# Re-spacing the mixing steps between the expert rows of a two-layer decoder on one Trainium2 core

## The chip, the core and the metric

The kernel runs on one core of one Trainium2 chip. The metric is the time of the whole launch in microseconds on the device: 1575.68 us for the kernel before, the median of three runs (1574.5 to 1578.08). TensorE, VectorE, ScalarE, GpSimd and SyncE are called PE, DVE, ACT, POOL and SP, as in the profile.

## The reference, cut to what matters

Two layers over 256 tokens of width 1024 (two tiles of 128 tokens). Each layer first mixes tokens (pooling and attention, gated, projected), then retrieves for each token 8 x 16 = 128 single-neuron experts from a table of 16384 and adds their outputs.

```python
def hybrid_layer(x, ...):
    h = rmsnorm(x, g_mix)
    z = h @ w_in                                  # pooling input, q, k, v, gate logits
    merged = gates[..., :D_MODEL] * branch_a + gates[..., D_MODEL:] * branch_b
    x = x + merged @ w_out
    return x + peer_ffn(rmsnorm(x, g_ffn), ...)

def peer_ffn(x, w_q, sub_keys, u, v):             # for each chunk of 128 tokens
    q = (xc @ w_q).reshape(TOKEN_CHUNK, PEER_HEADS, 2, PEER_HALF)
    s = jnp.einsum('thpd,pkd->thpk', q, sub_keys)
    sv, si = lax.top_k(s, PEER_TOPK)              # 16 best keys of each half
    ...                                           # 16 best sums give the expert ids eid and g
    act = jax.nn.gelu(jnp.einsum('thkd,td->thk', u[eid], xc))
    y = jnp.einsum('thk,thkd->td', g * act, v[eid])
```

## The kernel before

The work is four **windows** (layer 0 tile 0, layer 0 tile 1, layer 1 tile 0, layer 1 tile 1). A window's retrieval is 128 **rows**. Row g brings, for each of the 128 tokens, one expert's u and v vectors (2048 floats a token, 1 MiB a row) into one of the 7 slots of `ring`. Two rows make a **tick**, 64 ticks make a window, so there are 512 rows and 256 ticks.

What a row passes through:
- POOL issues an indirect DMA (line 1316), in order. It first waits until the slot's previous user, row g-7, has been summed.
- DVE computes the dot product with `tok` (`dot`, line 1181), ACT turns it into a weight through a GELU (lines 877 to 885).
- The v half is then summed in one of two ways. Row 0 of a tick listed in the set `shared` is summed on DVE (`weighted`, line 1194), behind the other row's dot. Every other row is summed on PE: ACT writes a diagonal (line 895), PE multiplies with it into two accumulating banks (`tensor_row`, line 675). That count, 382 rows on PE and 130 on DVE, is the same with and without the change.

The **mixing** of window w+1 and the search for its experts are cut into steps and slipped between the rows of window w. Each engine has a generator of steps for each window (`tensor_mix`, `scalar_mix`, `scalar_tops`, `vector_mix`); a step yields the tick at which it is due, and `streamed` emits row after row and, behind each, every step that has come due. So the order on each engine is fixed when the program is built. `when(w, tick)` turns a window's own tick into a tick of the program:

```python
def when(w, tick):
    return TICKS * (w - 1) + MIX_START + tick
```

The steps that matter here, with their ticks in `CHUNK_TICKS` and elsewhere:
- Ticks 5 to 26: projections with 1 MiB weight chunks (q, k, v, pooling input, gates, attention output), line 476 and others. SP loads chunks into two slots of `wring`; a load waits until the chunk two places earlier has been used. Twelve chunks of a layer stay in `held`.
- Ticks 31 to 35.5: output projection. `EASY` names ticks around it that are in `shared`.
- Ticks 42 to 63, every 3: eight **queries** pq0 to pq7 (line 476, 16 matmuls each, then two `score` matmuls, line 649, two ticks later). Behind pq5, PE spreads the gain row over all partitions (`everywhere`, line 398), which `hand_over` needs.
- `later_heads`: eight **heads** on DVE. Each has six steps: key search (lines 924 to 930) in two parts, search of the sums (lines 938 to 952) in two parts, picking of the ids (lines 971 to 985) in two parts.

Window 0's own steps have literal ticks (`first_heads`, `first_queries`).

At the first tick of a window (64, 128, 192) DVE runs `hand_over` (line 1173), which makes the new window's `tok` from x and the spread gain, ahead of the window's first dot; and behind the second dot `close` (line 1202) adds the PE banks to the old window's x. PE waits for `close` before it sums rows of the new window.

```python
def vector_row(dve, t, r):
    w, n = t // TICKS, t % TICKS
    if r == 0:
        for was in rows_on_vector(t - 1) if t else ():
            weighted(dve, t - 1, was)
        if n == 0:
            hand_over(dve, w)
    dot(dve, 2 * t + r)
    if r and n == 0 and w:
        close(dve, w - 1)
```

## Time and profile before

| what | value |
|---|---|
| median of three runs | 1575.68 us (1574.5 to 1578.08) |
| the profiled execution's own time | 1575.04 us |
| its span | 1573.3 us |
| PE, DVE, ACT, POOL busy | 82%, 73%, 58%, 42% of the span |
| moved by DMA | 643.51 MB, 409 GB/s over the span |
| first expert row's load | 103 us after the start |

The page gives busy shares of each engine, then the span in 40 slices with the rate of the DMA engines. The view of windows gives the same for stretches of one's own choice. The timeline lists instructions in order: start, length, engine, line, what it writes and reads, how often, and in brackets how long the engine had been idle before it and what ended that. All times are microseconds from the start of the span.

### The profile page before, as it was taken

The page shows a single profiled execution, that of the slowest core. Times are in us where ns is not written, and L with a number is a line of the kernel's source. Part 1 is how long each engine was busy: PE and PEld are TensorE (multiplying, and loading weights), DVE is VectorE, ACT ScalarE, POOL GpSimd, SP SyncE. Part 2 cuts the span into 40 slices and gives each one's busy share as a digit, 9 for nine tenths or more (in the row PEclk, how much of TensorE's full clock was granted, in tenths as well). Part 3 has the DMA queues.
Part 4 walks back from the last instruction along what each step waited for, and adds up shares of the span by engine and source line. Part 5 has one row for each costly group of instructions (what it writes and reads, how often), then busy time and mean ns, then how long its engine had stood idle before and what let it go on. Part 6 is the DMA issues. An engine that isn't in the chain of part 4 may idle for free.

```text
span 1573.3 us, 18796 instructions
## 1 busy us (share of the span) xinstructions
PE 1284.6 (82%) x5582; PEld 788.0 (50%) x5582; DVE 1149.6 (73%) x2692; ACT 914.3 (58%) x3307; POOL 662.0 (42%) x516
## 2 busy tenths in 40 slices
PE   8999898886898788766688978797778888787875
PEld 8986566543554556533355546564445542222321
DVE  2159998877888869636778887976778777777545
ACT  2236566557667546434676664655676666666676
POOL 0014344455445333223554433335554445554552
PEclk9999999997999899986899989999999999999999
DMA  9979999999999999999999999999999999999997
GB/s 393 397 320 401 408 413 420 421 421 422 402 389 408 421 420 421 421 421 419 421 417 410 396 417 422 419 420 421 421 418 416 396 410 421 421 421 421 421 420 292
DMA packets 89742, 643.51 MB, mean 409 GB/s; under 512 B 9976, under 2 KB 10536, under 8 KB 11816
## 3 DMA queue, kind: packets, MB, share of 16 engines
q0 software_dynamic: 73728, 536.90, 82.8%
q1 hardware_dynamic: 15588, 105.18, 16.2%
q8 instruction: 44, 0.72, 0.2%
q14 instruction: 58, 0.48, 0.1%
q10 hardware_dynamic: 324, 0.23, 0.0%
HBM read 641.23 MB, written 1.05 MB: 408 GB/s over the span
## 4 chain that ended last, share of the span: by engine, by line
DMA 43%; PE 26%; DVE 18%; ACT 6%; issue 5%; POOL 2%; SPq 0%; DVEq 0%; POOLq 0%; ACTq 0%
DMA ring<-in_uv,expert 41%; PE ybank L675 13%; PE bank L476 9%; DVE ring L1181 7%; DVE xs L1194 2%; POOL ring L1316 2%; DMA wring<-in_chunks 2%; PE bank L622 1%; ACT wgt L885 1%; ACT diag L895 1%; PE bank L611 1%; ACT th L883 1%; DVE buf L974 1%; DVE picked L977 1%; DVE si L930 1%
## 5 line engine op out<-in xcount | busy, mean ns | idle before, releaser
L1316 POOL DMA_INDIRECT ring<-in_uv,expert x512 | 661.8, 1293 | 890.8 <-PE ybank L675 546.2
L675 PE MATMUL ybank<-ring,diag 128*128 128x512 f32 x1528 | 790.7, 653 | 260.7 <-ACT diag L895 259.8
L1181 DVE SCALAR_TENSOR_TENSOR ring<-ring,tok 128x1024 f32<-128x1024 f32 x512 | 624.4, 1224 | 311.3 <-DMA ring<-in_uv,expert 305.8
L675 PEld LDWEIGHTS ybank<-ring,diag 128*128 128x128 f32 x1528 | 282.4, 200 | 654.6 <-ACT diag L895 417.7
L877 ACT ACTIVATE sq<-dots 128x1 f32<-128x1 f32 x512 | 102.8, 201 | 512.2 <-DVE ring L1181 511.2
L885 ACT ACTIVATE wgt<-th,half_p 128x1 f32<-128x1 f32 x512 | 198.1, 387 | 17.1
L476 PEld LDWEIGHTS bank<-hT,wring 128*128 128x128 f32 x1536 | 186.0, 199 | 35.1 <-issue 31.0
L476 PE MATMUL bank<-hT,wring 128*128 128x128 f32 x1536 | 186.8, 282 | 8.4 <-DMA wring<-in_chunks 8.1
L1194 DVE SCALAR_TENSOR_TENSOR xs<-ring,wgt,xs 128x1024 f32<-128x1024 f32 x128 | 164.0, 1282 | 5.2 <-ACT wgt L885 3.7
L895 ACT ACTIVATE diag<-cst,wgt 128x128 f32<-128x128 f32 x382 | 153.4, 402 | 15.9 <-PE ybank L675 3.6
L883 ACT ACTIVATE th<-arg,dots 128x1 f32<-128x1 f32 x512 | 150.8, 295 | 16.6
L878 ACT ACTIVATE half_p<-dots,prob 128x1 f32<-128x1 f32 x512 | 142.8, 279 | 0.2
L880 ACT ACTIVATE arg<-sq,gelu_bias 128x1 f32<-128x1 f32 x512 | 142.9, 279 | 0.0
L476 PEld LDWEIGHTS bank<-hT,held 128*128 128x128 f32 x736 | 91.5, 202 | 13.5 <-issue 13.5
L476 PE MATMUL bank<-hT,held 128*128 128x128 f32 x736 | 90.6, 284 | 0.0
L622 PE MATMUL bank<-held,buf 128*128 128x256 f32 x256 | 59.0, 385 | 0.0
L622 PEld LDWEIGHTS bank<-held,buf 128*128 128x128 f32 x256 | 49.9, 196 | 13.8 <-issue 7.4
L476 PE MATMUL bank<-hT,ring 128*128 128x128 f32 x448 | 51.1, 276 | 0.2 <-DMA ring<-in_chunks 0.2
L476 PEld LDWEIGHTS bank<-hT,ring 128*128 128x128 f32 x448 | 50.4, 192 | 0.9 <-DMA ring<-in_chunks 0.6
L686 ACT ACTIVATE buf<-bank 128x256 f32<-128x256 f32 (+2 forms) x65 | 28.5, 446 | 32.8 <-PE bank L476 30.1
L1181 DVE DVE_READ_ACCUMULATOR ring<-ring,tok 128x1 f32 x512 | 42.1, 82 | 0.0
L930 DVE FIND_INDEX8 si<-sv,buf 128x8 uint32<-128x128 f32 x128 | 34.9, 284 | 0.0
(126 smaller groups left out, 791.8 us busy)
## 6 DMA issues: line engine op xcount, KB each, us to landing
wring<-in_chunks SPq DMA_DIRECT2D x52, 1024.0 KB, 9.6
held<-in_chunks SPq DMA_DIRECT2D x24, 1024.0 KB, 24.8
ring<-in_chunks SPq DMA_DIRECT2D x20, 1024.0 KB, 12.0
ring<-in_uv,expert POOLq DMA_INDIRECT x512, 11.9
xs<-in_x SPq DMA_DIRECT2D x2, 512.0 KB, 4.3
wpool<-in_w_pool SPq DMA_DIRECT2D x2, 512.0 KB, 13.4
trunk_out<-buf SPq DMA_DIRECT2D x4, 256.0 KB, 4.8
ring<-in_pool_scale SPq DMA_DIRECT2D x1, 512.0 KB, 14.3
```

Source lines behind the costliest of these rows:

```text
L476: ins = pe.matmul(b[:, m * CW + lo:m * CW + lo + P], wt[k][:, lo:lo + P], hT[:, k, :], start=(k == 0), stop=(k == KC - 1))
L622: ins = pe.matmul(b[:, 0:CW], mergedT[:, k, :], wt[k][:, :], start=(k == 0), stop=(k == KC - 1))
L675: ins = pe.matmul(ybank[m][:, :], diag[:, nth % DIAGS, :], ring[:, (2 * t + r) % RING, D + m * BANK:D + (m + 1) * BANK], start=(nth == ten ...
L877: act_stepped(act.activation(sq[:, r:r + 1], dots[:, c:c + 1], ACT.Square))
L878: act.activation(half_p[:, c:c + 1], dots[:, c:c + 1], ACT.Copy, scale=prob[:, 2 * n + r:2 * n + r + 1])
L880: act_stepped(act.activation(arg[:, r:r + 1], sq[:, r:r + 1], ACT.Identity, scale=0.044715 * GELU_C, bias=gelu_bias[:, 0:1]))
L883: act_stepped(act.activation(th[:, r:r + 1], arg[:, r:r + 1], ACT.Tanh, scale=dots[:, c:c + 1]))
L885: ins = act.activation(wgt[:, c:c + 1], th[:, r:r + 1], ACT.Identity, scale=half_p[:, c:c + 1], bias=half_p[:, c:c + 1])
L895: act.activation(diag[:, nth % DIAGS, :], ident, ACT.Copy, scale=wgt[:, c:c + 1]).then_inc(diag_done, 1)
L1181: dve.scalar_tensor_tensor(out=ring[:, g % RING, 0:D], in0=ring[:, g % RING, 0:D], scalar=1.0, in1=tok[:, :], op0=ALU.mult, op1=ALU.mult, ...
L1194: dve.scalar_tensor_tensor(out=total, in0=ring[:, (2 * t + r) % RING, D:2 * D], scalar=wgt[:, c:c + 1], in1=total, op0=ALU.mult, op1=ALU.a ...
L1316: pool.indirect_dma_start(ring[:, g % RING, :], None, uv, bass.IndirectOffsetOnAxis(ap=expert[:, at:at + 1], axis=0)).then_inc(row_landed[ ...
```

## The change

Steps of windows 1 to 3 go through a piecewise linear map of their tick. Ticks up to 5 stay; 5 to 10 become 5 to 12.5 (1.5 apart for each 1), 10 to 24 become 12.5 to 28.5, 24 to 42 become 28.5 to 45 (closer), 42 to 63 become 45 to 64.5 (2.79 apart where it was 3), and what is later moves by 1.5. Mix, queries, scores and heads all go through it. The rows, `hand_over`, `close` and window 0's own steps don't. `EASY` moves by 3, and the ticks of chunks in `shared` follow the map.

```diff
-EASY = range(29, 46)
+EASY = range(32, 49)
...
+        paces = ((-99, -99), (5, 5), (10, 12.5), (24, 28.5), (26, 30.5), (31, 34), (35.5, 38.5), (42, 45), (63, 64.5),
+                 (163, 164.5))
+
+        def paced(tick):
+            for (a, at), (b, bt) in zip(paces, paces[1:]):
+                if tick <= b:
+                    return at + (tick - a) * (bt - at) / (b - a)
+
         def when(w, tick):
-            return TICKS * (w - 1) + MIX_START + tick
+            return TICKS * (w - 1) + MIX_START + (paced(tick) if w else tick)
...
-        shared |= {when(w, n) for w in range(1, windows) for n in EASY} | {ceil(n) for n in first_queries}
+        shared |= {TICKS * (w - 1) + MIX_START + n for w in range(1, windows) for n in EASY}
+        shared |= {ceil(n) for n in first_queries}
```

From `rows_on_tensor` on, line numbers of the changed kernel are higher by 10. Three places show what moves.

**PE, around the gain of window 1** (ticks 60 to 66). L476 is a query, L398 the gain, L649 a score, L675 rows (4 to a tick where both rows are PE's). Before:

```order
L476 MATMUL bank<-hT,held 128x128 x16
L398 MATMUL bank<-gains,cst 128x128 x8
L675 MATMUL ybank<-ring,diag 128x512 x8
L649 MATMUL bank<-beside,buf 128x128 x2
L675 MATMUL ybank<-ring,diag 128x512 x2
L476 MATMUL bank<-hT,wring 128x128 x16
L675 MATMUL ybank<-ring,diag 128x512 x6
```

With the change:

```order
L486 MATMUL bank<-hT,held 128x128 x16
L408 MATMUL bank<-gains,cst 128x128 x8
L685 MATMUL ybank<-ring,diag 128x512 x6
L659 MATMUL bank<-beside,buf 128x128 x2
L685 MATMUL ybank<-ring,diag 128x512 x2
L486 MATMUL bank<-hT,wring 128x128 x16
L685 MATMUL ybank<-ring,diag 128x512 x8
```

Before, pq5 and the gain stand behind row 1 of tick 60, and the last two of the rows up to pq6 belong to tick 63. Now they stand behind row 1 of tick 62, with two PE rows (tick 63) left before the new window; pq6 has moved from tick 63 to 65.

**DVE, at the hand-over of window 1** (tick 64). L1181 is a dot, L1194 a row summed on DVE, L1173 `hand_over`, L1202 `close`, L971 to L977 a pick. Before:

```order
L1181 SCALAR_TENSOR_TENSOR ring,dots<-ring,tok 128x1024 x2
L1194 SCALAR_TENSOR_TENSOR xs<-ring,wgt,xs 128x1024
L1173 SCALAR_TENSOR_TENSOR tok<-xs,stat,bank 128x512 x2
L1181 SCALAR_TENSOR_TENSOR ring,dots<-ring,tok 128x1024
L971 TENSOR_TENSOR buf<-cabf,cst 128x256
L974 TENSOR_TENSOR buf<-buf,sif 128x256
L977 TENSOR_REDUCE picked<-buf 128x16
L1181 SCALAR_TENSOR_TENSOR ring,dots<-ring,tok 128x1024
L1202 TENSOR_TENSOR xs<-xs,ybank 128x512 x2
```

With the change:

```order
L1204 SCALAR_TENSOR_TENSOR xs<-ring,wgt,xs 128x1024
L1191 SCALAR_TENSOR_TENSOR ring,dots<-ring,tok 128x1024 x2
L1183 SCALAR_TENSOR_TENSOR tok<-xs,stat,bank 128x512 x2
L1191 SCALAR_TENSOR_TENSOR ring,dots<-ring,tok 128x1024
L948 TENSOR_TENSOR buf<-sv 128x256
L950 CAST sif<-si 128x32
L937 MAX cv<-buf 128x8
L940 MAX_INDEX ci<-cv,buf 128x8
L1191 SCALAR_TENSOR_TENSOR ring,dots<-ring,tok 128x1024
L1212 TENSOR_TENSOR xs<-xs,ybank 128x512 x2
```

`hand_over` and `close` have kept their places among the dots; tick 63 is no longer in `shared` (no L1204 between the last dots), and the search of the sums has taken the pick's place.

**DVE, tick 12 of window 0**, where window 1's normalisation (L1014, L1021) meets a key search of window 0 (L924 to L930). Before:

```order
L1014 COPY buf<-bank 128x128
L1021 SCALAR_TENSOR_TENSOR hT<-bank,cst,buf 128x128 x4
L1181 SCALAR_TENSOR_TENSOR ring,dots<-ring,tok 128x1024
L924 MATCH_REPLACE buf<-sv,buf 128x128 x2
L927 MAX sv<-buf 128x8 x2
L930 MAX_INDEX si<-sv,buf 128x8 x2
L1021 SCALAR_TENSOR_TENSOR hT<-bank,cst,buf 128x128 x4
L1194 SCALAR_TENSOR_TENSOR xs<-ring,wgt,xs 128x1024
```

With the change, at tick 14:

```order
L1191 SCALAR_TENSOR_TENSOR ring,dots<-ring,tok 128x1024
L1024 COPY buf<-bank 128x128
L1031 SCALAR_TENSOR_TENSOR hT<-bank,cst,buf 128x128 x4
L1191 SCALAR_TENSOR_TENSOR ring,dots<-ring,tok 128x1024
L1031 SCALAR_TENSOR_TENSOR hT<-bank,cst,buf 128x128 x4
L1204 SCALAR_TENSOR_TENSOR xs<-ring,wgt,xs 128x1024
```

The key search stays at tick 12, and the normalisation now stands by itself two ticks later.

## Rows read from the trace of the kernel before

**Rows 1.** The page: the span, and the DMA rate in 40 slices.
```profile
span 1573.3 us, 18796 instructions
...
GB/s 393 397 320 401 408 413 420 421 421 422 402 389 408 421 420 421 421 421 419 421 417 410 396 417 422 419 420 421 421 418 416 396 410 421 421 421 421 421 420 292
```

**Rows 2.** Windows: stretch, length, busy by engine, granted PE clock, DMA share, GB/s.
```profile
120.00:240.00 120.00, 102.49 (x557) 71.96 (x555) 113.74 (x310) 69.89 (x264) 49.43 (x40) 0.95 1.00 408
240.00:400.00 160.00, 130.18 (x580) 81.69 (x581) 124.89 (x242) 98.78 (x357) 77.42 (x58) 0.89 1.01 421
400.00:480.00 80.00, 72.31 (x305) 44.66 (x305) 69.20 (x178) 51.22 (x193) 37.05 (x30) 0.94 0.98 389
...
800.00:880.00 80.00, 70.66 (x321) 44.15 (x320) 70.74 (x184) 51.71 (x196) 37.62 (x31) 0.98 0.99 401
880.00:1160.00 280.00, 225.78 (x1038) 144.85 (x1037) 218.73 (x479) 164.63 (x594) 121.92 (x93) 0.92 1.01 420
1160.00:1280.00 120.00, 103.40 (x427) 62.20 (x426) 96.41 (x226) 80.23 (x298) 59.26 (x48) 0.97 1.00 406
...
```

**Rows 3.** Timeline of POOL: row loads issued after long waits.
```profile
188.53 1.68 POOL L1316 DMA_INDIRECT ring<-in_uv,expert  x1 [5.78 <-DVE xs L1194]
...
420.10 0.94 POOL L1316 DMA_INDIRECT ring<-in_uv,expert  x1 [4.48 <-PE ybank L675]
...
436.65 1.86 POOL L1316 DMA_INDIRECT ring<-in_uv,expert  x1 [5.29 <-PE ybank L675]
...
470.21 0.94 POOL L1316 DMA_INDIRECT ring<-in_uv,expert  x1 [5.55 <-PE ybank L675]
...
870.30 1.02 POOL L1316 DMA_INDIRECT ring<-in_uv,expert  x1 [6.02 <-PE ybank L675]
...
1236.82 1.89 POOL L1316 DMA_INDIRECT ring<-in_uv,expert  x1 [5.80 <-PE ybank L675]
```

**Rows 4.** The row load in the view of line 1316: from issue to landing.
```profile
DMA to landing us min/median/max: 5.7/11.9/29.9
```

**Rows 5.** Timeline of PE at the end of window 0: pq5, the gain, four rows.
```profile
461.95 4.10 PE L476 MATMUL bank<-hT,held 128*128 128x128 f32 x32
465.98 2.04 PE L398 MATMUL bank<-gains,cst 24*128 24x128 f32 x16
467.96 7.13 PE L675 MATMUL ybank<-ring,diag 128*128 128x512 f32 x16
```

**Rows 6.** Timeline of DVE at the hand-over to window 1.
```profile
472.13 1.28 DVE L1194 SCALAR_TENSOR_TENSOR xs<-ring,wgt,xs 128x1024 f32<-128x1024 f32 x1
473.33 1.40 DVE L1173 SCALAR_TENSOR_TENSOR tok<-xs,stat,bank 128x512 f32<-128x512 f32 x2
474.76 1.23 DVE L1181 SCALAR_TENSOR_TENSOR ring<-ring,tok 128x1024 f32<-128x1024 f32 x1
...
478.43 1.28 DVE L1202 TENSOR_TENSOR xs<-xs,ybank 128x512 f32<-128x512 f32 x2
```

**Rows 7.** Timelines of PE and DVE at the hand-over to window 3: gain, hand-over.
```profile
1232.59 2.05 PE L398 MATMUL bank<-gains,cst 24*128 24x128 f32 x16
...
1241.51 1.40 DVE L1173 SCALAR_TENSOR_TENSOR tok<-xs,stat,bank 128x512 f32<-128x512 f32 x2
```

**Rows 8.** Timeline of ACT: a weight's first and last instruction.
```profile
461.18 0.20 ACT L877 ACTIVATE sq<-dots 128x1 f32<-128x1 f32 x1 [2.05 <-DVE ring L1181]
...
462.53 0.40 ACT L895 ACTIVATE diag<-cst,wgt 128x128 f32<-128x128 f32 x1
```

**Rows 9.** Timeline of DVE: search of the sums, first part; the dot behind; second part; the next dot.
```profile
463.78 0.42 DVE L938 TENSOR_TENSOR buf<-sv 128x256 f32<-128x256 f32 x1
...
465.32 1.23 DVE L1181 SCALAR_TENSOR_TENSOR ring<-ring,tok 128x1024 f32<-128x1024 f32 x1
...
466.47 0.09 DVE L924 MATCH_VALUE_LOAD buf<-cv,buf 128x8 f32 x1
...
468.54 1.22 DVE L1181 SCALAR_TENSOR_TENSOR ring<-ring,tok 128x1024 f32<-128x1024 f32 x1
```

## The prediction

> **What bounds the kernel now.** I read the page's row of DMA rates first, then windows around its dips, then the timeline of POOL inside them. The rate stands at 420 to 422 GB/s in most slices [rows 1], and at 420 to 421 over the long windows 240 to 400 and 880 to 1160 [rows 2], while no engine is busy all the time there (PE 81%, DVE 78% of the window from 240). So the transfers bound the kernel: a row of 1 MiB (1.049 MB) takes 1.049 / 421 = 2.49 us, a tick without weights 4.98 us. The change moves the same bytes. It can only change the time in which the DMA engines run below that rate. I count this shortfall as length x (1 - rate / 421): 3.7 us in 120 to 240, 6.1 in 400 to 480, 3.8 in 800 to 880, 4.3 in 1160 to 1280 [rows 2], 17.9 us in all. The start and the last slice are left as they are.
>
> In these dips POOL sits idle before a load, because the slot's previous row has not been summed [rows 3]. In the three later windows I count eight such waits of 3.9 us or more, of which the rows show five. Their shortfall is 6.1 + 3.8 + 4.3 = 14.2 us, so **a wait costs 1.8 us**. The pattern is the same at each: a query holds PE for about 4 us, or 6.1 us with the gain behind it, and up to four rows then leave in one burst [rows 5]. The seven slots turn round in 7 x 2.49 = 17.4 us when the rate is full; a load takes 5.7 us even at its shortest [rows 4] and POOL over 1 us to issue, so a slot that is held more than some 10 us after its landing leaves the DMA engines short.
>
> **The change part by part.** No operation is added or removed; 382 rows stay on PE and 130 on DVE. So only the places count.
>
> 1. Ticks 12 to 28 of window 0 (from 180 us). The wait of 5.78 us [rows 3] ends with a DVE sum that stood behind a key search and half of window 1's normalisation. With the change tick 12 has no such sum and the normalisation comes two ticks later, so this wait should go. But the chunk loads also leave this stretch, which is what kept DMA fed while DVE was busy 95% of the time [rows 2], and DVE still has window 0's searches. At best both this wait and the smaller one after it go (-3), at worst nothing is won (0). I take **-1.0 us**, nearer the worse end because of that 95%.
>
> 2. Dense projections of windows 2 and 3 (from 520 and 900 us). They now come 1.5 ticks apart and the DMA rate was already 420 there [rows 2]. A later chunk load moves bytes from one full stretch to another: **0**. The cover is the queue of gathers itself; if PE waited for a late chunk, its price would be at most one wait, 1.8. SP reloads the layer's side table behind the last score, which comes 1.5 ticks later, but the first q chunk is used at the same tick 72; I expect this to fit, and put 1.8 into the upper bound.
>
> 3. Ticks 42 to 63, queries. Before, each query came behind row 1 of a `shared` tick, so PE's next four rows queued behind it. Now pq3 and pq4 come ahead of row 1 of a `shared` tick: the next PE row is two dots (5 us) later, and a query of 4.1 us [rows 5] is nearly covered. The waits behind pq3 (436.65 in rows 3), behind pq4 in the two later windows and behind the last query of window 3 should go: 4 x 1.8 = **-7.2 us**. The wait behind pq2 (420.10) stays, for its surroundings are the same. Bounds: two of the four go (-3.6), or pq2's three go as well (-12.6).
>
> 4. **The hand-over.** Before, the gain was on PE from 465.98 to 468.02 [rows 5], and DVE took it at 473.33 [rows 6]: 5.3 us to spare. The gain now stands four rows nearer to `hand_over`, which has not moved: 4 x 2.49 = 10.0 us. So DVE will wait 4.7 us for PE, at a place where every later dot stands behind the wait. A second way to it, from the start of the last dot of tick 62: dot 1.2, then 0.6 + 2.05 us until the diagonal is there (the weight runs from 461.18 to 462.93 [rows 8], behind a short handing over), 1.8 for the PE row, 4.1 for pq5 and 2.0 for the gain [rows 5] give 11.1 to 11.7. DVE meanwhile does a dot, a key search (taken at the length of a sums search, 1.5 to 2.1 [rows 9]), a sum and two dots, 1.2 each, and is there at 6.6. The wait is 4.5 to 5.1. At window 3 the spare was 1241.51 - 1234.64 = 6.9 us [rows 7], leaving 3.1 of wait.
>
>    What queues behind it: `hand_over` 1.4, dot 1.2, search of the sums 1.5, dot, `close` 1.3 [rows 6], second part of the search 2.1 [rows 9], and only then the DVE sum of tick 64's row 0. That is some 21 us behind the start of the reference dot, so that slot is held about 15 us after landing; and pq6, now at tick 65, holds four more rows. I expect POOL to wait three times of 5 us or more at windows 1 and 2 (behind the gain, behind the sum of tick 64, behind pq6) where there was one, and twice at window 3. At window 2, one chunk load for the next window, set free by pq6, fills part of a gap. New waits: 2 + 1.5 + 1 = 4.5, times 1.8 is **+8.1 us**. The wait behind the gain itself also lasts longer, as PE has only two rows to give back before DVE goes on: about 6.7 us where it was 5.55 [rows 3], +1.1 at two windows and +0.5 at the third, **+2.7 us**. Bounds: the ring hides the stall and only half a wait is new at each window (+2.7), or each window pays the full 15 - 10 = 5 us and 1.8 more for pq6, less the 1.8 it paid before (3 x 5 = +15).
>
> The sum: -1.0 + 0 - 7.2 + 8.1 + 2.7 = **+2.6 us** on the profiled execution's 1575.04 us, which is 0.6 below the median shown. That gives 1577.6; I give 1577.5.
>
> **A page against the trace.** The shortest landing of a row in the trace is 5.7 us behind its issue [rows 4]. The Trainium skill, page "DMA: Bandwidth & Descriptors", section on the anatomy of one DMA on the GpSimd path, gives a fixed 2.0 us plus the bytes at 436 GB/s, an estimate of 4.4 us for such a row. By that, a starved ring would be refilled 1.3 us sooner, a wait would cost 0.5 rather than 1.8 us, and part 4 would come to some +3 us, so the kernel would get slightly faster. The 1.8 is read off this kernel's own dips, so I keep it.
>
> **The rivals.** About 3 us (0.2%) is what a measurement of this kernel can tell from no change.
>
> - *The ring takes up the stall* (faster). DVE waits at the hand-over but has spare time around it (DVE is busy 86% in 400 to 480 [rows 2]), the rows landed meanwhile are dotted in one go, and only part 4's lower bound is paid. Then -1.0 - 7.2 + 2.7 = -5.5: 1569.5 us. For it: the rate is full again soon after 480, in the slice behind the dip [rows 1]. Against it: the next sums on DVE stand behind 10 us of work. It decides where POOL's wait behind tick 64's sum stays under about 4 us.
> - *The stall at the hand-over runs on* (slower). The place is `hand_over` at ticks 64, 128, 192; the price the upper bound of part 4, +15 against -1.0 and -7.2: 1575 + 6.8 = 1582 us. For it: DVE's wait, `close` and PE's wait for `close` follow each other, and pq6 comes before the ring has recovered. Against it: window 3 has no head steps there. It decides once DVE's wait for the gain passes 4 us and the slot of tick 64 is held over 12 us.
> - *It does nothing*: the steps slide within a stretch that DMA fills, and shortfalls only change place. Then 1575 us. Against it are the four waits of part 3, which have a cause in the order.
>
> **How the numbers follow.** Forecast (gains and the hand-over roughly cancel) 0.45; ring takes it up 0.25; stall runs on 0.25; nothing 0.05. Of the forecast's own range, 1571.5 to 1581.5, most lies within 0.2% of before. That gives same 0.40 (0.31 from the forecast, 0.04 from the ring, 0.05 from nothing), faster 0.24 (0.03 and 0.21), slower 0.36 (0.11 and 0.25). The range 1568 to 1585 reaches both rivals' values with 1.5 to 3 us beyond each.
>
> **What would show it.** In the changed kernel's profile: `hand_over` (L1183) with DVE idle 4 to 5 us before it, ended by PE's gain (L408), at windows 1 and 2, and about 3 at window 3. POOL waits of 5 us or more in a row of three from there on. The rate in the slices before it (ticks 54 to 60) nearer to 421 (the slices there showed 402 and 389 [rows 1]). The dip near 180 us smaller. If DVE doesn't wait at L1183, part 4 is wrong and the kernel is faster; if the dips behind pq3 and pq4 remain, part 3 is wrong and it is slower. If dense projections fall below 415 GB/s, part 2 is wrong.

## The result and the profile after

The changed kernel takes 1586.41 us (median of eight runs, 1580.53 to 1587.31), the kernel before 1576.06 us (eight runs, 1574.47 to 1578.08) on the same chip. The ratio is **1.0056 (95% interval 1.0040 to 1.0072)**, or some 8.8 us slower. By that ratio on the 1575.68 us that stood ahead of the prediction it is 1584.5, at the upper end of the forecast's range; the median itself lies 1.4 us beyond it. The sign of the sum (slower) is right; its size (+2.6 us) is not. The profiled execution took 1586.77 us with a span of 1585.0 us, 11.7 more than the span in [rows 1]. The eight runs fall into five at 1586.05 to 1587.31 (granted clock 0.927 to 0.934) and three at 1580.53 to 1582.97 (0.935 to 0.942), and the profiled one is of the upper five, so sums over its rows explain 11.7 us, not 8.8; whether the clock is the cause of the difference or follows from it isn't known.

The page of the changed kernel: its span, and the rate of the DMA engines in 40 slices.

```profile
span 1585.0 us, 18803 instructions
...
GB/s 392 390 317 419 407 404 420 421 422 421 420 418 315 420 421 421 420 422 421 421 420 407 352 405 416 421 418 421 421 421 419 387 406 421 421 421 421 422 413 296
```

A slice is some 40 us. In [rows 1] the two slices before 475 us were at 402 and 389, and the one from 475 at 408. Now they are at 420 and 418, and the one behind them is at 315. The same at 880 us: 352 where 396 was the lowest. So the time is not lost where the queries stand now, but directly behind the hand-over.

Windows of the kernel before around the three hand-overs, each stretch cut at the hand-over's beginning (columns as in rows 2), and two that the experiments below are compared with:

```profile
400.00:469.00 69.00, 61.31 (x257) 37.96 (x257) 59.55 (x162) 44.38 (x166) 30.75 (x24) 0.93 0.99 400
469.00:500.00 31.00, 27.66 (x115) 16.40 (x114) 28.58 (x70) 19.99 (x76) 16.21 (x13) 0.94 0.96 388
800.00:874.00 74.00, 64.66 (x285) 39.74 (x284) 64.88 (x174) 48.59 (x185) 33.31 (x28) 0.98 0.98 401
874.00:906.00 32.00, 27.50 (x116) 16.54 (x115) 26.93 (x68) 20.17 (x73) 16.64 (x14) 0.95 1.01 420
1160.00:1235.00 75.00, 64.51 (x287) 40.34 (x286) 61.23 (x145) 51.42 (x191) 37.40 (x29) 0.98 1.01 410
1235.00:1270.00 35.00, 29.08 (x115) 17.45 (x114) 26.93 (x62) 21.48 (x80) 16.13 (x13) 0.95 1.00 406
...
480.00:560.00 80.00, 63.50 (x267) 38.73 (x266) 66.53 (x176) 46.51 (x167) 35.35 (x27) 0.89 1.01 422
...
880.00:960.00 80.00, 62.82 (x268) 38.00 (x267) 67.18 (x177) 47.79 (x170) 32.56 (x26) 0.91 1.01 421
```

Windows of the changed kernel, cut in the same way, with the stretch of part 1 (120 to 240), and the dense projections from 916:

```profile
120.00:240.00 120.00, 104.01 (x542) 69.21 (x540) 113.71 (x321) 70.45 (x263) 53.27 (x42) 0.99 1.01 409
...
400.00:476.00 76.00, 65.18 (x302) 40.41 (x302) 61.91 (x159) 50.58 (x181) 36.65 (x29) 0.98 1.01 419
476.00:506.00 30.00, 22.32 (x84) 12.93 (x83) 28.37 (x69) 16.29 (x63) 11.15 (x9) 0.89 0.76 283
...
800.00:882.00 82.00, 69.44 (x302) 42.67 (x303) 67.50 (x168) 54.37 (x196) 38.77 (x31) 0.94 1.01 414
882.00:916.00 34.00, 27.53 (x121) 17.48 (x121) 29.81 (x72) 19.47 (x73) 12.86 (x11) 0.85 0.86 326
916.00:960.00 44.00, 36.35 (x159) 22.36 (x159) 35.85 (x97) 27.11 (x96) 17.05 (x15) 0.92 1.01 413
1160.00:1256.00 96.00, 79.45 (x334) 46.36 (x333) 76.47 (x169) 65.06 (x235) 46.77 (x37) 0.92 1.01 420
1256.00:1286.00 30.00, 25.61 (x109) 15.93 (x108) 25.36 (x56) 19.86 (x76) 14.31 (x11) 0.94 0.93 356
```

With the prediction's measure, length x (1 - rate / 421), the shortfalls are:

| stretch | before, us | after, us | difference | predicted |
|---|---|---|---|---|
| 120 to 240 (part 1) | 3.7 | 3.4 | -0.3 | -1.0 |
| queries ahead of the three hand-overs (part 3) | 3.4 + 3.5 + 2.0 = 8.9 | 0.4 + 1.4 + 0.2 = 2.0 | **-6.9** | -7.2 |
| hand-overs (part 4) | 2.4 + 0.1 + 1.2 = 3.7 | 9.8 + 7.7 + 4.6 = 22.1 | **+18.4** | +10.8 |
| dense part, 916 to 960 (part 2; before: 880 to 960, at 421) | 0 | 0.8 | +0.8 | 0 |

The sum is +12.0 us, against 11.7 between the two spans. Both kernels move 643.51 MB, so over the whole span the shortfalls must differ by just that: the count shows where the time went, not why. Two smaller stretches stand outside the table: 1270 to 1300, with the wait behind the last query of window 3, was at 408 GB/s (0.9 us short) and 1286 to 1300 is now at 422; 0 to 120, where the change moves no step, went from 371 to 367 (1.1 us). In 476 to 506 PE is busy for 22.3 us of the 30, ACT for 16.3, and the DMA engines 76%. DVE has 28.4 us of work in it, but its dots come late.

DVE's idle time before `hand_over` in the changed kernel's view of waits (sum, count, longest):

```profile
DVE tok L1183 <- PE bank L408: 14.0, 3, 5.0
```

DVE's timeline at the three hand-overs: `hand_over`, the first dot of tick 64, and the DVE sum of tick 64's row 0. It answers to [rows 6, 7].

```profile
476.18 1.53 DVE L1183 SCALAR_TENSOR_TENSOR tok<-xs,stat,bank 128x512 f32<-128x512 f32 x2 [4.99 <-PE bank L408]
477.74 1.23 DVE L1191 SCALAR_TENSOR_TENSOR ring<-ring,tok 128x1024 f32<-128x1024 f32 x1
...
484.85 1.29 DVE L1204 SCALAR_TENSOR_TENSOR xs<-ring,wgt,xs 128x1024 f32<-128x1024 f32 x1
...
883.03 1.53 DVE L1183 SCALAR_TENSOR_TENSOR tok<-xs,stat,bank 128x512 f32<-128x512 f32 x2 [4.83 <-PE bank L408]
...
1254.87 1.53 DVE L1183 SCALAR_TENSOR_TENSOR tok<-xs,stat,bank 128x512 f32<-128x512 f32 x2 [4.15 <-PE bank L408]
```

PE's timeline from the last rows of window 0 on (it answers to [rows 5]): pq5, the gain, the two rows of tick 63, then four matmuls of a row of tick 64, and pq6.

```profile
470.81 4.13 PE L486 MATMUL bank<-hT,held 128*128 128x128 f32 x32
474.88 2.04 PE L408 MATMUL bank<-gains,cst 24*128 24x128 f32 x16
476.85 3.70 PE L685 MATMUL ybank<-ring,diag 128*128 128x512 f32 x8
483.60 1.96 PE L685 MATMUL ybank<-ring,diag 128*128 128x512 f32 x4 [3.05 <-ACT diag L905]
...
490.63 3.78 PE L685 MATMUL ybank<-ring,diag 128*128 128x512 f32 x4 [4.63 <-ACT diag L905]
494.20 4.37 PE L486 MATMUL bank<-hT,wring 128*128 128x128 f32 x32
```

POOL's timeline (it answers to [rows 3]): the row loads that come behind a long wait at the first hand-over, and the longest at the other two.

```profile
479.11 1.02 POOL L1326 DMA_INDIRECT ring<-in_uv,expert  x1 [6.88 <-PE ybank L685]
...
486.41 1.68 POOL L1326 DMA_INDIRECT ring<-in_uv,expert  x1 [3.94 <-DVE xs L1204]
...
494.69 0.94 POOL L1326 DMA_INDIRECT ring<-in_uv,expert  x1 [2.78 <-PE ybank L685]
500.57 0.94 POOL L1326 DMA_INDIRECT ring<-in_uv,expert  x1 [4.95 <-PE ybank L685]
...
885.97 1.01 POOL L1326 DMA_INDIRECT ring<-in_uv,expert  x1 [6.52 <-PE ybank L685]
...
1257.80 1.81 POOL L1326 DMA_INDIRECT ring<-in_uv,expert  x1 [6.28 <-PE ybank L685]
...
1275.24 0.94 POOL L1326 DMA_INDIRECT ring<-in_uv,expert  x1 [5.08 <-PE ybank L685]
```

Read the three fences together. DVE is done with window 0's dots at 471.2 (476.18 less 4.99). `hand_over` is two instructions, each for one half of `tok` and of the gain: the first starts at 476.18, as soon as PE has done the gain's first half, and the second at 476.96, just behind the end of the gain at 476.92. No dot is made in 6.6 us, while in that time 2.6 rows could land. PE then has exactly two rows to give back (476.85 to 480.55), waits 3 us for the next diagonal, and after that row has little work until 490.63. POOL waits 6.88, 3.94, 2.78 and 4.95 us in 22 us. That is the chain the prediction drew; what it cost was new.

### The profile page after: what moved, and what is told of

The parts are those of the page before. It is cut to its first block, busy times and chain, and to the rows that moved or that the text cites. A ratio compares the mean times of both kernels' runs of the same rounds, so it can differ in the third digit from the quotient of the medians.

```text
span 1585.0 us, 18803 instructions
## 1 busy us (share of the span) xinstructions
PE 1287.1 (81%) x5582; PEld 787.3 (50%) x5582; DVE 1150.4 (73%) x2692; ACT 913.8 (58%) x3307; POOL 655.0 (41%) x516
## 2 busy tenths in 40 slices
DMA packets 89742, 643.51 MB, mean 406 GB/s; under 512 B 9976, under 2 KB 10536, under 8 KB 11816
## 3 DMA queue, kind: packets, MB, share of 16 engines
HBM read 641.23 MB, written 1.05 MB: 405 GB/s over the span
## 4 chain that ended last, share of the span: by engine, by line
DMA 40%; PE 26%; DVE 20%; issue 6%; ACT 6%; POOL 2%; DVEq 0%; POOLq 0%; ACTq 0%
DMA ring<-in_uv,expert 39%; PE ybank L685 13%; PE bank L486 9%; DVE ring L1191 7%; DVE xs L1204 3%; POOL ring L1326 2%; ACT wgt L895 1%; ACT diag L905 1%; ACT th L893 1%; PE bank L466 1%; PE bank L632 1%; DVE ci L940 1%; DVE buf L984 1%; DVE picked L987 1%; DVE si L940 1%
## 5 line engine op out<-in xcount | busy, mean ns | idle before, releaser
L1326 POOL DMA_INDIRECT ring<-in_uv,expert x512 | 654.8, 1279 | 909.5 <-PE ybank L685 557.6
L1204 DVE SCALAR_TENSOR_TENSOR xs<-ring,wgt,xs 128x1024 f32<-128x1024 f32 x128 | 164.1, 1282 | 6.8 <-ACT wgt L895 5.5
L486 PEld LDWEIGHTS bank<-hT,held 128*128 128x128 f32 x736 | 87.9, 196 | 10.7 <-issue 10.7
## 6 DMA issues: line engine op xcount, KB each, us to landing
ring<-in_chunks SPq DMA_DIRECT2D x20, 1024.0 KB, 11.7
```

The lines of the kernel that those rows point to most:

```text
L486: ins = pe.matmul(b[:, m * CW + lo:m * CW + lo + P], wt[k][:, lo:lo + P], hT[:, k, :], start=(k == 0), stop=(k == KC - 1))
L1204: dve.scalar_tensor_tensor(out=total, in0=ring[:, (2 * t + r) % RING, D:2 * D], scalar=wgt[:, c:c + 1], in1=total, op0=ALU.mult, op1=ALU.a ...
L1326: pool.indirect_dma_start(ring[:, g % RING, :], None, uv, bass.IndirectOffsetOnAxis(ap=expert[:, at:at + 1], axis=0)).then_inc(row_landed[ ...
```

## The experiments

Each run stands beside runs of the kernel before on the same chip; 0.2% (3 us) is again what a measurement can tell. The question was which part of the change carries the loss: the late gain, the queries pq6 and pq7 behind the hand-over, or the dense part; and whether the gain of part 3 exists.

### The gain moved forward by one query (e1)

```diff
-                if w and h == PH - 3:
+                if w and h == PH - 4:
```

> The changed kernel with the gain spread on PE behind pq4 instead of pq5, about 2.8 ticks earlier; all else the same. Theory A (the late gain makes DVE wait at the hand-over, and this wait is what the change costs): no wait of hand_over for the gain, and 1574 us (1571 to 1577), since the DMA shortfall behind ticks 64 and 128 falls from about 9 and 6 us to 3 each. Rival B (the crowding of pq6 and of head steps behind tick 64 costs it, the gain is a bystander): the wait goes, the time stays at 1583 to 1587 us.

Measured: 1576.38 us against 1575.11, ratio 1.0005 (0.9994 to 1.0015). The view of waits has no row for `hand_over` any more. With one line the loss of 0.56% is gone. Windows of this kernel:

```profile
400.00:480.00 80.00, 71.05 (x324) 44.67 (x322) 70.19 (x181) 53.12 (x192) 37.97 (x31) 0.97 1.01 414
480.00:560.00 80.00, 65.02 (x292) 41.77 (x290) 64.21 (x162) 47.92 (x172) 32.18 (x28) 0.89 0.97 393
800.00:880.00 80.00, 68.01 (x321) 42.45 (x319) 70.10 (x174) 54.04 (x196) 40.19 (x31) 1.00 1.01 413
880.00:960.00 80.00, 66.02 (x298) 41.69 (x298) 66.62 (x172) 48.15 (x173) 32.10 (x28) 0.91 0.99 397
```

**The late gain carries nearly the whole difference**: 1.0056 less 1.0005 is 0.51%, 8.0 us. But the kernel isn't faster than before either, although part 3's gain ahead of the hand-over is still there (414 where [rows 2] had 389). The stretches behind the hand-over are at 393 and 397, where they had 422 and 421 before. What is left there must have another cause; e10 and e11 look for it.

### A late gain alone, twice (e2 and e7)

e2, in the kernel before, sets the gain off from pq5 and puts it behind tick 62, so that it stands late by itself:

```diff
                 if w and h == PH - 3:
+                    yield when(w, 59)
                     pe.wait_ge(gains_in, 16 * (layer + 1))
```

> The kernel before, with nothing changed but the gain spread, which PE does two ticks later (behind row 1 of tick 62 instead of tick 60). Theory A: hand_over waits 3 to 5 us at windows 1 and 2, some 2 at window 3, and the time rises by 4 to 8 us to 1580 to 1584. Rival B: the wait appears, and the time stays within 2 us of 1576, or falls, because the 6.1 us block of pq5 and gain is split.

Measured: 1575.96 us against 1575.11, ratio 1.0002 (0.9992 to 1.0012). The wait hardly came about:

```profile
DVE tok L1174 <- PE bank L398: 0.7, 1, 0.7
```

Away from the query the gain is a block of only 2.05 us [rows 7], and PE had caught up by then. So this run says nothing on the price of a wait. (Its rates moved all the same, with every query at its old tick: 400 to 480 went from 389 to 411 GB/s and 480 to 560 from 422 to 405. We come back to this at e5.) It does say that lateness in ticks is not what counts; the 4.1 us query directly ahead of the gain is part of it.

e7, in the kernel before, moves the gain ahead of pq6, behind tick 63:

```diff
-                yield from cols_by(C_PQ + h, f"pq{h}", 1)
-                if w and h == PH - 3:
+                if w and h == PH - 2:
+                    yield when(w, 60)
                     pe.wait_ge(gains_in, 16 * (layer + 1))
                     everywhere(pe, w, G_FFN, "gain")
+                yield from cols_by(C_PQ + h, f"pq{h}", 1)
```

> The kernel before with the gain spread alone moved behind row 1 of tick 63, just ahead of pq6. The run with the gain at tick 62 gave no wait to speak of (0.7 us once), so it did not test the price of one; this one must: hand_over waits 4 to 5 us at each window. Theory A (the wait costs time by itself): 1580 to 1584 us. Rival B (a DVE wait at this place is taken up by the ring unless pq6 and head steps are also moved to it): within 2 us of 1576.

Measured: 1582.66 us against 1575.42, ratio **1.0049 (1.0034 to 1.0063)**, 7.7 us. Its row of waits, and POOL's longest wait at the first hand-over:

```profile
DVE tok L1174 <- PE bank L398: 14.2, 4, 5.6
```

```profile
485.51 1.68 POOL L1317 DMA_INDIRECT ring<-in_uv,expert  x1 [9.66 <-DVE xs L1195]
```

The same 14 us of waiting as in the changed kernel, with the other steps at their old ticks (only pq6 now queues behind the gain, some 2 us later), costs the same as the late gain did there (8.0 us): 0.55 us of run time for each microsecond that DVE waits. Two edits from two sides, one that takes the wait from the changed kernel and one that gives it to the kernel before, agree. Here the POOL wait ends with the DVE sum of tick 64, the step named in the prediction as late next. (The profiled execution is the shortest of its five runs, 1579.99 us, so its rates show less than the median.)

### Queries and output projection alone (e4)

```diff
-        paces = ((-99, -99), (5, 5), (10, 12.5), (24, 28.5), (26, 30.5), (31, 34), (35.5, 38.5), (42, 45), (63, 64.5),
+        paces = ((-99, -99), (26, 26), (31, 34), (35.5, 38.5), (42, 45), (63, 64.5),
```

> The old ticks up to 26 and those of the change from 31 on (queries, heads and gain later, closer). Theory A: 1586 us (1582 to 1589), the whole loss, with the 4 to 5 us waits of hand_over. Rival C: 1576 to 1579 us.

Measured: 1584.95 us against 1575.11, ratio 1.0059 (1.0046 to 1.0072). That is the whole loss, so no share of the dense part shows in it. `hand_over` waits 16.9 us in three times here, up to 6.2, which is more than in the changed kernel; a gain of a microsecond or so by the dense part can't be told from this run.

### The dense part alone (e3 and e8)

e3 kept the changed `EASY` and let the map come back to the old ticks at 45, ticks 43 to 45 crowded:

```diff
-        ... (35.5, 38.5), (42, 45), (63, 64.5),
-                 (163, 164.5))
+        ... (35.5, 38.5), (42, 43), (45, 45),
+                 (163, 163))
```

> The spacing of the change up to tick 42, and the old ticks from 45 on (queries, scores, heads, gain as before); three rows more are summed on PE. Theory A: 1575 us (1572 to 1577), a little below before by the stall at 190 us. Rival C (spacing the dense projections costs the time by itself, by leaving DMA unfed): 1580 us or more, with dips between 500 and 650 us.

Measured: 1578.89 us against 1575.11, ratio 1.0020 (1.0011 to 1.0028). The dense stretches are full (421 GB/s in 480 to 560 and in 880 to 960), and the loss is in the queries' stretches: 391 in 800 to 880 where [rows 2] had 401. The edit was not clean. `EASY`'s ticks in `shared`, with their additional DVE sums, now reached three ticks into the unmoved heads; 385 rows instead of 382 were on PE. e8 repeats it with `EASY = range(29, 46)` as before and a map that is back at the old ticks from 42 on (391 rows on PE):

```diff
-EASY = range(32, 49)
+EASY = range(29, 46)
...
-        ... (31, 34), (35.5, 38.5), (42, 45), (63, 64.5),
-                 (163, 164.5))
+        ... (31, 33), (35.5, 36.5), (42, 42),
+                 (163, 163))
```

> The spacing of the change up to tick 26 only, drawn back to the old ticks by 42, EASY as before, so that from tick 45 on all is the kernel before; 9 rows more are summed on PE. The first run of this kind also moved EASY, so that DVE sums met head steps in ticks 49 to 51. Theory A: 1574.5 us (1573 to 1576.5). Rival C (spacing the dense part costs by itself): 1578 us or more, as in that run.

Measured: 1574.62 us against 1575.42, ratio 0.9992 (0.9981 to 1.0003): no difference that can be told. Part 2 costs nothing that shows, and parts 1 and 2 together give some 1.3 us, which is not told from zero. e3's 3.8 us therefore belong to the late part of its edit: the moved `EASY`, the crowded ticks 43 to 45, or both. The two weren't separated.

### Does the queries' gain exist? (e5 and e6)

Part 3 rests on queries standing ahead of row 1 of their tick. e5 does that to all eight queries, pq6 and pq7 among them, in the kernel before, by half a tick, so that the gain is not late (the scores go along, the heads don't):

```diff
-               42, 45, 48, 51, 54, 57, 60, 63)
+               41.5, 44.5, 47.5, 50.5, 53.5, 56.5, 59.5, 62.5)
```

> The kernel before with its eight queries of windows 1 to 3 half a tick earlier (41.5, 44.5 ... 62.5), so that each stands ahead of PE's row of a shared tick, whose other row is DVE's, instead of behind it; pq5's gain goes with it. Theory A, part 3 (a query ahead of a shared tick delays one PE row little, one behind it delays four): 1571 us (1568 to 1573), the dips at 400 to 480 and 1160 to 1280 smaller. Rival D (the place within the tick is of no account, only the number of queries): 1574 to 1578 us.

Measured: 1573.72 us against 1575.42, ratio 0.9992 (0.9984 to 1.0001). Its windows:

```profile
400.00:480.00 80.00, 70.11 (x301) 41.33 (x300) 70.95 (x185) 51.20 (x192) 36.40 (x31) 0.98 1.01 420
480.00:560.00 80.00, 63.14 (x257) 39.20 (x256) 66.07 (x171) 48.02 (x173) 35.58 (x27) 0.84 1.00 404
800.00:880.00 80.00, 70.76 (x310) 42.04 (x309) 70.82 (x185) 51.93 (x196) 37.09 (x31) 1.00 1.01 415
880.00:960.00 80.00, 62.52 (x271) 39.24 (x270) 66.10 (x174) 47.77 (x170) 33.59 (x27) 0.94 1.01 415
960.00:1160.00 200.00, 162.19 (x760) 106.65 (x758) 151.95 (x303) 116.95 (x426) 84.04 (x67) 0.91 1.01 416
...
1160.00:1300.00 140.00, 121.75 (x462) 66.58 (x463) 112.31 (x268) 93.85 (x350) 67.89 (x56) 0.98 1.01 419
```

The gain in front exists: the first dip of 389 GB/s is gone (420), by an edit of half a tick. In the stretches ahead of the hand-overs of windows 1 and 2 it wins 6.1 + 3.8 - 0.2 - 1.1 = 8.6 us, and in 1160 to 1300 (409 before, 419 now) 3.3 more. But 480 to 560 falls from 422 to 404 (3.4 us), 880 to 960 from 421 to 415 (1.1 us) and 960 to 1160 from 420 to 416 (1.9 us); 1300 to 1540 falls from 421 to 419 (1.1 us). Of 11.9 us won, 1.6 are left between the two spans and 1.3 between the run times. Some 7.5 us are found again in these rows, and the rest in small amounts elsewhere: 1.5 us behind 1540, and 1.5 us in all in 0 to 240 and 560 to 800, where a step of 1 GB/s already counts for 0.3 to 0.6 us. **A shortfall removed in front of the hand-over largely comes back elsewhere, 4.5 us of it in the 80 us behind the first two hand-overs.** That is the prediction's rival with 0.05, *it does nothing*, for this term alone.

Why it comes back isn't shown. One reason could be that pq6 and pq7 moved too and stand worse beside the hand-over. e2 speaks against that as the only reason: there no query moved, and 480 to 560 fell just the same (405) when 400 to 480 rose (411). No run moves pq0 to pq5 half a tick and leaves pq6 and pq7.

e6 is e5 with `yield when(w, 58)` ahead of the gain.

> As the run before, and the gain spread by itself behind row 1 of tick 61, so that no block of 6.1 us stands on PE. Theory A: no wait of hand_over (2 us to spare), one burst less, 1569 us (1566 to 1572), the fastest of all. Rival: as the run before or slower, since the gain comes nearer to the hand-over.

Measured: 1574.10 us against 1575.42, ratio 0.9994 (0.9985 to 1.0003). It adds nothing: with pq5 half a tick earlier than before, the gain is not late, and there was no wait to remove.

### What is left behind the hand-over (e10 and e11)

Both start from e1. e10 moves the steps from tick 60 on further out, to bring pq6 and pq7 away from the hand-over:

```diff
-                if w and h == PH - 3:
+                if w and h == PH - 4:
...
-        ... (42, 45), (63, 64.5),
-                 (163, 164.5))
+        ... (42, 45), (57, 58.9), (60, 62), (63, 65),
+                 (163, 165))
```

> The changed kernel with the gain behind pq4 (so no wait of hand_over for it), and the steps from tick 60 on half a tick later, so that pq6 and pq7 and the scores between them stand farther from the hand-over. The gain moved alone gave 1576.4 us, with 393 GB/s still in 480 to 560. My theory: what is left of that dip is pq6 standing too near the hand-over, so 480 to 560 rises to 400 or more and the kernel comes to about 1574 us. Rival: the dip is carried by POOL's wait behind the first query after the hand-over wherever it stands, and it stays near 393 GB/s with 1576 us.

Measured: 1577.14 us against 1576.13, ratio 1.0008 (0.9999 to 1.0017). 480 to 560 didn't rise, though my theory said it would:

```profile
480.00:560.00 80.00, 64.62 (x296) 41.32 (x295) 62.79 (x160) 46.56 (x167) 31.36 (x26) 0.91 0.96 389
```

But the edit doesn't do what it was made for. `streamed` sets steps off only behind a row, so every half tick, and pq6's old tick of 64.71 and its new one of 65 both come due behind row 1 of tick 65. PE's timeline has it in the same place as in e1: behind the score and one row of tick 65, with four rows behind it. Only pq7 and its score, and head steps from there on, are one row later. So e10 leaves the theory on pq6 untested, although its numbers are those of the rival.

e11 puts pq6 and pq7, their scores and heads back to the ticks of the kernel before, and pays with queries 2.5 ticks apart in front:

```diff
-        ... (42, 45), (63, 64.5),
-                 (163, 164.5))
+        ... (42, 45), (60, 60), (63, 63),
+                 (163, 163))
```

> The changed kernel with the gain behind pq4 and the map running from 42 -> 45 back to 60 -> 60, so pq6 and pq7, their scores and heads stand at the ticks of the kernel before, and pq0 to pq5 are 2.5 ticks apart. With the gain moved alone, 480 to 560 had 393 GB/s, 880 to 960 had 397, against 422 and 421 before. My theory: pq6 and pq7 later beside the hand-over carry what is left there, so both stretches are back at 415 or more; queries 2.5 ticks apart cost something before the hand-over (400 to 480 at 405 to 415), and the time is 1572 to 1576 us. Rival: the dip behind the hand-over comes from how full the ring is on arriving there and not from pq6 and pq7, so it stays under 405 GB/s.

Measured: 1575.37 us against 1575.23, ratio 0.9997 (0.9988 to 1.0006). Its windows:

```profile
400.00:480.00 80.00, 71.50 (x352) 46.88 (x351) 73.02 (x187) 54.04 (x196) 37.85 (x31) 0.98 1.00 405
480.00:560.00 80.00, 64.99 (x266) 38.55 (x266) 64.25 (x173) 46.82 (x169) 32.84 (x27) 0.90 1.00 409
800.00:880.00 80.00, 70.05 (x339) 45.53 (x338) 72.67 (x184) 53.72 (x195) 38.39 (x32) 0.98 0.99 402
880.00:960.00 80.00, 65.73 (x284) 40.13 (x282) 66.53 (x178) 49.41 (x177) 34.56 (x28) 0.94 1.01 416
```

Neither side is quite right. The stretches behind the hand-over rise from 393 and 397 to 409 and 416, one of them short of the 415 I asked for, so the last two queries, with the scores and heads that moved with them, do carry most of what was left there. Which of these it is wasn't separated. The stretches in front fall from 414 and 413 to 405 and 402. The shortfalls of the four stretches are 12.7 us in e1, 9.9 in e11 and 9.7 in the kernel before, and the run times of all three lie within 0.1%. Together with e5 this says that where the queries stand decides **where** the rate falls, while the run time stays within 3 us.

### A version that beats both (e9)

e8's spacing of the dense part, e5's queries half a tick earlier, and the gain set off at its own tick 58 (tick 61 of window 0, as in e6):

```diff
-               42, 45, 48, 51, 54, 57, 60, 63)
+               41.5, 44.5, 47.5, 50.5, 53.5, 56.5, 59.5, 62.5)
...
-EASY = range(32, 49)
+EASY = range(29, 46)
...
-        ... (31, 34), (35.5, 38.5), (42, 45), (63, 64.5),
-                 (163, 164.5))
+        ... (31, 33), (35.5, 36.5), (40.5, 40.5),
+                 (163, 163))
...
+                    yield when(w, 58)
```

> The changed kernel with its wide spacing of the dense steps kept, the map back to identity at tick 40.5, all eight queries half a tick earlier than before, and the gain set apart at tick 58. My theory: the dense spacing is worth 0 to -1 us and the queries half a tick earlier -1 to -2 us, and they add, so about 1573 us (1571.5 to 1574), 2 to 3 us below the kernel before, with no wait of hand_over for the gain and 418 GB/s or more in 400 to 480. Rival: the two only move shortfalls about and do not add: 1574 to 1576 us, no difference. If the wait for the gain came back through the new step it would be 1580 or more.

Measured: 1572.79 us (eleven runs) against 1576.13 (twenty), ratio **0.9981 (0.9971 to 0.9990)**: 3.0 us faster than the kernel before. The interval excludes 1, though the difference is just short of the 0.2% named above. Against the changed kernel it is 0.75% faster (0.9981 / 1.0056). Its windows:

```profile
400.00:480.00 80.00, 70.04 (x299) 41.05 (x298) 71.00 (x185) 50.42 (x190) 34.66 (x31) 0.98 1.01 421
480.00:560.00 80.00, 63.34 (x264) 37.92 (x262) 62.52 (x167) 47.45 (x170) 34.31 (x28) 0.91 0.99 403
```

The two small gains (0.9992 each, which would make 0.9984) are compatible with adding up. That they add isn't shown: the interval overlaps that of e5 (0.9984 to 1.0001) and that of e8 (0.9981 to 1.0003). In front of the first hand-over the rate is full (421; 418 in 800 to 880), and what is left is again just behind it (403).

## Why the prediction was right or wrong

**What bounds the kernel: right.** The transfers bound it, no long stretch of either kernel passed 422 GB/s, and what the change cost went into the three stretches at the hand-overs (283, 326 and 356 GB/s). (That the count gives 12.0 us where the spans differ by 11.7 is no further proof: the bytes are the same.)

**Part 1** (-1.0 us): right, mechanism and size. The wait of 5.78 us near 188 [rows 3] is gone as said, the longest there now being 3.19, and 180 to 200 went from 388 to 421 GB/s. In this pair of profiles the whole stretch, 120 to 240, gave only -0.3 us (408 to 409). But thirteen kernels were profiled, and seven of them have these steps at the new ticks: they show 421 to 424 in 180 to 200, the six with the old ticks 368 to 395. Over 120 to 240 the seven are at 409 to 412 and the six at 405 to 408, in the mean 410.1 against 407.0, which is 0.9 us.

**Part 2** (0): right; e8 agrees, at 0.9992 (0.9981 to 1.0003). 916 to 960 is at 413 in the changed kernel and so just below the 415 set as the sign that part 2 is wrong; it costs 0.8 us, next to the hand-over's dip.

**Part 3** (-7.2 us): right in its stretches (-6.9 us). Of the waits of 3.9 us or more there, the ones behind pq3 and pq4 and the one at window 3's last query are gone. The wait behind pq2, which was to stay, is down from 4.48 to 3.45 at window 1 and up from 3.46 to 4.71 (at 842) at window 2. One reading was wrong: at window 2 the wait that was to go (3.92 at 836.81) stands behind pq3, not pq4. What part 3 left out, e5 shows: a shortfall removed in front of a hand-over is for the most part paid elsewhere. The weak step is the tacit one from "this wait should go" to "its 1.8 us are won".

**Part 4** (+8.1 and +2.7): the mechanism was right, the price was not.

| | predicted | measured |
|---|---|---|
| DVE's wait at windows 1, 2, 3 | 4.7, 4.7, 3.1 us | 4.99, 4.83, 4.15 us |
| POOL's wait behind the gain at windows 1, 2, 3 | 6.7, 6.7, 6.3 us | 6.88, 6.52, 6.28 us |
| last dot of tick 62 (464.64) to tick 64's DVE sum | some 21 us | 20.2 us |
| long POOL waits at windows 1, 2, 3 | 3, 3, 2 of 5 us or more | 1, 1, 2 of 5 us or more; 3, 3, 2 of 3.9 us or more |
| shortfall at the hand-overs | +10.8 us, bounds +2.7 to +15 | **+18.4 us** |

That DVE's wait came out so near at windows 1 and 2 is in part luck. The prediction counted to the end of the gain. By that measure DVE stood 5.7, 5.6 and 4.9 us ahead of it (471.19 against 476.92 at window 1), about 1 us more than predicted at the first two and 1.8 us at the third, and at window 1 the rows say where it comes from: PE began pq5 6.2 us behind the start of the reference dot (464.64 to 470.81), not 5.0 to 5.6, while DVE was there at 6.6 as counted. `hand_over` needs only the gain's first half to start, which the prediction left out, and that gave 0.7 us back.

The mis-sized term is **"a wait costs 1.8 us"**, 14.2 us over eight waits. At the hand-overs there are eight waits again (the fence above shows six; the others are 3.94 and 4.63 us at window 2), with 22.1 us of shortfall: 2.8 us each. And the trace of before had waits of that length that cost nothing. Between 510 and 575 POOL waits five times for 4.0 to 5.5 us, with the rate at 420 over that stretch; this is the longest (timeline of POOL, kernel before), and below it the DMA queues of that stretch, the row loads in q0 and SP's loads in q1 (packets, MB, share):

```profile
552.05 1.06 POOL L1316 DMA_INDIRECT ring<-in_uv,expert  x1 [5.49 <-PE ybank L675]
...
q0 software_dynamic: 2660, 19.34, 71.7%
q1 hardware_dynamic: 1226, 7.92, 29.4%
```

So POOL's wait is no unit of loss. But the rows of the queues show what stood beside these free waits: SP's loads, nearly all of them weight chunks, don't pass through the ring and moved 29% of the bytes. Between 240 us and 1500 us, outside the dips, every POOL wait of 3.9 us or more in the kernel before falls into a stretch with chunk loads (240 to 293, 505 to 740, 880 to 1076); in 740 to 800, with row loads alone at 420 GB/s, no wait reaches 3 us. At the changed kernel's hand-overs there is one chunk load at the second (1.05 MB in 882 to 916) and none at the other two. One wait is nearly free without chunk loads: 5.38 us at 1511.60, with 412 GB/s in 1510 to 1520 (0.2 us short), some 0.5 MB of output stores beside it. It comes by itself behind 200 us of full rate. So two conditions go with a cheap wait, other loads in the queues and a ring that is full when it begins, and which weighs how much isn't shown. At a hand-over neither holds: the second and the fourth wait follow within 22 us of the first, and the rate in steps of 2 us goes to 78 GB/s (478 to 480), back to 426 (482 to 484), and down again to 98 (486 to 488) and 135 (500 to 502), where the dip behind pq3 in the kernel before, a single wait of 5.29 us, had 234 at its lowest (438 to 440). That the ring was still short of rows at the later waits is argued from this; rows under way weren't counted.

The upper bound of 15 us was too low as well: it charged one stall of (15 - 10) = 5 us for a window and pq6 an ordinary 1.8, and left pq7 out. e1 divides the 18.4 us: the wait for the gain is worth 8.0 us of run time, and with it gone the stretches behind the first two hand-overs still lack 5.3 and 4.6 us, which e11 lays mostly to pq6 and pq7 with their scores and heads, and which part 3's gain about pays for.

**Which case it was.** *The stall at the hand-over runs on* is what happened, at its place (ticks 64, 128, 192) and past its first mark (a gain wait over 4 us, each time). Its time was 1582; measured against the profiled execution it is 1586.8, and 1583.9 by the ratio on 1575.04. The forecast, at 0.45, treated this as an even match of gains and losses by taking the middle price for part 4. The chances of 0.36 for slower and 0.24 for faster leaned the right way, and not enough. *The ring takes up the stall* was wrong: the ring took up some 6 of the 14 us that DVE waited, and the rest came out as time. *It does nothing* fits the queries alone (e1, e5, e11), and not the change.

**The page against the trace.** The prediction kept 1.8 us for a wait against the Trainium skill, page "DMA: Bandwidth & Descriptors", section on the anatomy of one DMA, by whose 2.0 us plus bytes at 436 GB/s a wait would have cost an estimated 0.5. The shortest row load took 5.7 us in the trace of before, where that rule gives 4.4. At the hand-overs the runs go further from that rule: 2.8 us of shortfall a wait, and 7.7 us of run time for the gain's waits alone (e7), while beside chunk loads a wait cost nothing that shows. A rule for a single transfer takes account neither of what else is in the queues nor of how many slots of the ring are empty at once. One thing was wrong in the prediction's own sum by that rule: it put 0.5 into part 4 only. With 0.5 for every wait parts 1, 3 and 4 come to -0.3, -2.0 and +3.0, so +0.7 us, which is no change and not "slightly faster".

## What to carry to other kernels

- Before you move a step towards a point where the engines hand over to one another, count the slack of what that point waits for. Here it was 5.3 us, and the move took 10 by the count and 11 as measured. The wait came out within 0.3 us of the count at two hand-overs (in part by luck) and 1.1 us above it at the third, and one line (the gain one query earlier) takes the loss away.
- Don't price a stall by dividing a shortfall by a count of long waits. Look for the same wait in a full stretch first (here 5.5 us for nothing), ask what else kept the DMA engines busy there (here weight chunks, 29% of the bytes), and where stalls follow each other before the ring is full again, bound each by its full length.
- In a stream bound by transfers, a dip that is smoothed in one place can come back at the next obstacle. Don't count it as won before a run of that edit alone has shown it (here 1.3 of 11.9 us were left in e5).
- One pair of profiles is too few for a term of 1 us. Part 1 looked like -0.3 us in one pair and is -0.9 over the thirteen kernels profiled.
- Where steps are set off only between rows, look in the order of instructions whether an edit of a fraction of a tick moved anything (pq6 in e10 stayed).

## What the runs showed of the hardware that I had not expected

- Half a tick (2.5 us) decides over a whole dip: e5 moves eight queries by that and 400 to 480 goes from 389 to 420 GB/s, while 480 to 560 goes from 422 to 404.
- DVE's idle time before `hand_over` translates into run time at nearly the same rate in two different kernels: 14.0 us into 8.0 (changed kernel less e1) and 14.2 us into 7.7 (e7).
- `hand_over` itself takes 1.53 us behind a wait for PE, and 1.40 without one [rows 6]. Its second half starts at 476.96, just behind the end of the gain at 476.92, so it waits for the gain's second half once more.
- POOL waits of 4.0 to 5.5 us cost nothing while chunk loads share the DMA engines: 420 GB/s in 510 to 575, with 19.34 MB of row loads and 7.92 MB of others. The row loads alone reach the same rate (420 in 740 to 800).
